# A two-layer diffusion trunk on one Trainium2 core: a shorter opening, 64-row products, and stationary expert weights

## The reference, cut to what matters

```python
def _trunk(x, cvec, P, caches):
    for l in range(DEPTH):
        mod = (jax.nn.silu(cvec) @ P['w_ada'][l] + P['b_ada'][l])[:, None, :]
        sh1, sc1, g1, sh2, sc2, g2 = jnp.split(mod, 6, axis=-1)
        mix, ctx_tensors = _token_mixer(x * (1.0 + sc1) + sh1, P, l, ctx)
        x = _layer_norm(DN_ALPHA * x + g1 * mix, P['ln1_g'][l], P['ln1_b'][l])
        h = x * (1.0 + sc2) + sh2
        f = _dense_ffn(h, P, l // 2) if l % 2 == 0 else _moe_ffn(h, P, l // 2)
        x = _layer_norm(DN_ALPHA * x + g2 * f, P['ln2_g'][l], P['ln2_b'][l])

def _moe_ffn(h, P, i):
    ...
    for e in range(N_EXPERTS):
        y = (jax.nn.silu(xt @ P['moe_w_gate'][i, e]) * (xt @ P['moe_w_up'][i, e])) @ P['moe_w_down'][i, e]
        out = out + gates[:, e:e + 1] * y
```

## Time and profile before

| | us |
|---|---|
| median of 3 runs (lowest, highest) | 2065.25 (2064.94, 2067.51) |
| the profiled execution | 2065.61 |
| its span, first to last instruction | 2063.8 |
| start of the first projection | 49.34 |
| start of the experts' weight transfers | 1144.25 |

### The profile page before, as it was taken

How to read it: one execution, slowest core, us unless ns; L and a number is a source line. 1 busy time by engine, 2 the same in 40 slices (tenths; PEclk the granted TensorE clock), 3 DMA queues, 4 the chain that set the end, 5 groups by cost and what they waited for, 6 DMA issues and landing times.

```text
span 2063.8 us, 25323 instructions
## 1 busy us (share of the span) xinstructions
PE 1962.5 (95%) x10904; PEld 1457.8 (71%) x10904; DVE 464.5 (23%) x984; ACT 253.3 (12%) x525; POOL 11.6 (1%) x24
## 2 busy tenths in 40 slices
PE   6999899998999989989998999999999999999996
PEld 3776668887888868788887766666666666577653
DVE  0244334222000033555333200000111000200103
ACT  0121113101000012221301100000000000000001
POOL 0000000000000000000000000000000000000000
PEclk8999999999999999999998899999999999999999
DMA  9436463323334343201230899999999999988794
GB/s 394 170 116 245 166 245 139 128 102 123 152 133 168 133 157 123 93 24 42 82 104 0 334 421 421 421 420 421 421 421 421 421 420 422 421 328 297 264 419 171
DMA packets 73565, 510.95 MB, mean 248 GB/s; under 512 B 9202, under 2 KB 10674, under 8 KB 11892
## 3 DMA queue, kind: packets, MB, share of 16 engines
q1 hardware_dynamic: 72820, 508.76, 62.3%
q0 software_dynamic: 640, 0.66, 0.1%
HBM read 507.68 MB, written 1.70 MB: 247 GB/s over the span
## 4 chain that ended last, share of the span: by engine, by line
PE 55%; DMA 5%; DVE 2%; ACT 0%; SPq 0%; issue 0%; ACTq 0%; DVEq 0%
PE bank L583 22%; PE bank L1037 10%; PE bank L1051 7%; DMA area<-in_moe 5%; PE bank L1061 5%; PE bank L904 3%; PE bank L788 1%; PE bank L773 1%; PE bank L1072 1%; PE bank L927 1%; PE bank L1044 1%; SPq L499 0%; PE bank L752 0%; PE bank L778 0%; PE bank L753 0%; DVE area L1463 0%
## 5 line engine op out<-in xcount | busy, mean ns | idle before, releaser
L583 PE MATMUL bank<-hT,area 128*128 128x256 f32 (+1 forms) x2080 | 460.8, 382 | 9.4 <-DVE hT L1468 9.4
L583 PEld LDWEIGHTS bank<-hT,area 128*128 128x128 f32 (+1 forms) x2080 | 392.4, 190 | 73.1 <-issue 11.5
L583 PE MATMUL bank<-area,mixer 128*128 128x256 f32 (+1 forms) x1408 | 309.5, 375 | 1.0 <-ACT mixer L1417 1.0
L583 PEld LDWEIGHTS bank<-area,mixer 128*128 128x128 f32 (+1 forms) x1408 | 256.5, 188 | 51.1 <-issue 20.6
L1037 PE MATMUL bank<-area,mixer 128*64 128x256 f32 x2240 | 255.2, 381 | 4.4 <-DMA area<-in_moe 4.4
L1037 PEld LDWEIGHTS bank<-area,mixer 128*64 128x64 f32 x2240 | 160.7, 137 | 97.9 <-issue 29.8
L1463 DVE TENSOR_TENSOR hT<-hT,bank 128x256 f32<-128x256 f32 x154 | 64.8, 421 | 717.4 <-ACT hT L1394 579.5
L1051 PE MATMUL bank<-area,hT 128*128 128x512 f32 x336 | 154.1, 601 | 0.5 <-ACT hT L1424 0.5
L1061 PE MATMUL bank<-area,hT 128*64 128x512 f32 x560 | 127.6, 597 | 2.7 <-DMA area<-in_moe 2.2
L1051 PEld LDWEIGHTS bank<-area,hT 128*128 128x128 f32 x336 | 61.4, 190 | 72.4 <-issue 71.0
L596 PE MATMUL bank<-area,cS 128*32 128x256 f32 x768 | 92.8, 398 | 18.9 <-DMA area<-in_ada 18.9
(11 more groups left out here) (290 smaller groups left out, 1430.3 us busy)
## 6 DMA issues: line engine op xcount, KB each, us to landing
area<-in_moe SPq DMA_DIRECT2D x336, 1024.0 KB, 24.0
area<-in_mix SPq DMA_DIRECT2D x62, 1024.0 KB, 4.9
area<-in_ada SPq DMA_DIRECT2D x48, 1024.0 KB, 6.8
area<-in_dense SPq DMA_DIRECT2D x33, 1024.0 KB, 6.7
cst<-in_cst SPq DMA_DIRECT2D x1, 2125.5 KB, 11.6
xT<-in_xT SPq DMA_DIRECT2D x1, 1024.0 KB, 21.0
out_yT<-xT SPq DMA_DIRECT2D x4, 256.0 KB, 2.5
mixer<-in_wbB SPq DMA_DIRECT2D x2, 256.0 KB
```

Of the source, the lines that this page charges most:

```text
L583: last = mm(out, a, b, start=(n == 0), stop=(n == len(pairs) - 1), **kw)
```

## The change

1. The opening takes 8 tiles of w_ada instead of 12. The other 40 are 20 early pairs: the two new ones are in stream 1 of layer 0, ahead of the wait for the decays and ahead of the wait for `nu_ready`. The ring's slots are counted on from there.
2. The constants come in two transfers: 8 columns in the opening, the rest behind the tiles q0 and q1.
3. The scores and the RWKV matrices are products over 64 rows, one for each half of the partitions, into different PSUM banks. The zeroed copies go; VectorE writes `KR` with two plain multiplications instead of four, and the start state for both heads side by side.
4. x takes the start state of two heads in one product; y alternates between the two column halves.
5. In wide expert passes the weights are stationary and the 128 gathered tokens move. The hidden values come out with a feature per partition, so the transposes and the copies to `mhidT` go, and down waits for `moe_hid`.

```diff
-ADA_FIRST = ADA_TILES // 2
+ADA_FIRST = ADA_TILES // 3
...
-            ada_first(0)
-            ada_first(1)
-            for name, dst in [("cst", cst), ("xT", xT), ("bada", bada), ("lnp", lnp), ("rv", rv)]:
...
+            for n in range(RING):
+                ada_first(n)
+            sp.dma_start(cst[:, 0:8], ins["cst"][:, 0:8]).then_inc(sem("cst_in"), 16)
+            for name, dst in [("xT", xT), ("bada", bada), ("lnp", lnp), ("rv", rv)]:
+                sp.dma_start(dst[:], ins[name]).then_inc(sem("params_in"), 16)
...
+                    if l == 0 and i == 2:
+                        sp.dma_start(cst[:, 8:], ins["cst"][:, 8:]).then_inc(sem("cst_in"), 16)
...
                 for j in range(4):
-                    mm(bank[4 + j][:, :], qL[:, j, :], kxL[:, :, :], start=True, stop=True)
+                    for g in range(2):
+                        mm(bk(4 + 2 * g + j // 2, 2, 256)[:, j % 2, :], qL[64 * g:64 * g + 64, j, :],
+                           kxL[64 * g:64 * g + 64, :], start=True, stop=True)
                 for j in range(4):
-                    last = mm(bk(2 + j // 2, 2, 256)[:, j % 2, :], qT[:, j, 0:P], kxP[:, :, :], start=True, stop=True)
+                    for g in range(2):
+                        last = mm(bk(2 + g, 4, P)[:, j, :], qT[64 * g:64 * g + 64, j, 0:P],
+                                  kT[64 * g:64 * g + 64, 0:P], start=True, stop=True)
...
+                elif l == 0:
+                    early_pair()
                 pe.wait_ge(sem("decays_ready"), 2 * k)
...
                     for c in range(2):
-                        mm(bank[2 + c][:, :], Bc[d][:, c, :], KR[d][:, c, :, :, :], start=True, stop=True)
-                        mm(bank[4 + c][:, :], KcR[d][:, c, :], KR[d][:, c, :, :, :], start=True, stop=True)
+                        for first, source in ((2, Bc), (4, KcR)):
+                            for i in range(2):
+                                half = slice(64 * i, 64 * i + 64)
+                                mm(bk(first + i, 2, 256)[:, c, :], source[d][half, c, :], KR[d][half, c, :, :],
+                                   start=True, stop=True)
                     for c in range(2):
                         for i in range(2):
-                            last = mm(bk(6, 4, P)[:, 2 * c + i, :], KR[d][:, c, 0, i, :], Bc[d][:, c, :],
+                            half = slice(64 * i, 64 * i + 64)
+                            last = mm(bk(6 + i, 2, P)[:, c, :], KR[d][half, c, 0, :], Bc[d][half, c, :],
                                       start=True, stop=True)
...
+                        if st == 1:
+                            mm(bank[2 + d][:, P * c:P * c + P], KR[d][:, c, 0, :], s0c[:, 2 * d + c, :, :],
+                               start=True, stop=False, skip_group_check=True)
...
+                if st == 1 and l == 0:
+                    early_pair()
                 pe.wait_ge(sem("nu_ready"), 2 * k)
...
+                    for d in range(2):
+                        for source, weights in ((Vn[:, st, :], AKQ[d]), (nU[d], MTQ[d])):
+                            for i in range(2):
+                                h = 2 * c + i
+                                last = mm(out[64 * i:64 * i + 64], source[:, 64 * h:64 * h + 64], weights[:, c, 1, i, :],
+                                          start=(st == 0 and d == 0 and source is not nU[d]),
+                                          stop=(d == 1 and source is nU[d]), skip_group_check=True)
...
-                    acc(out, [(x[:, c, :], m8(tile)[:, c, :]) for c in range(KC)]).then_inc(done, 1)
+                    for h in range(2):
+                        last = acc(out[:, P * h:P * h + P],
+                                   [(m8(tile)[:, c, P * h:P * h + P], x[:, c, :]) for c in range(KC)])
+                    last.then_inc(done, 1)
...
-                            last = mm(bank[first_bank + h][:, :], mhidT[par][:, P * c:P * c + P],
+                            last = mm(bank[first_bank + h][:, :], mhid[par][:, P * c:P * c + P],
...
-                        turn_hidden(u % 2).then_inc(sem("moe_turned"), 1)
+                        if not is_wide(q):
+                            pe.wait_ge(sem("moe_hid"), u + 1)
+                            turn_hidden(u % 2).then_inc(sem("moe_turned"), 1)
...
-                    for i in range(2):
-                        v.scalar_tensor_tensor(KR[d][:, :, 0, i, :], kapT[:, :, cols], hm[:, i:i + 1],
-                                               Ep[d][:, :, 1, :], ALU.mult, ALU.mult)
-                        v.scalar_tensor_tensor(KR[d][:, :, 1, i, :], rT[:, :, cols], hm[:, i:i + 1],
-                                               Ep[d][:, :, 0, :], ALU.mult, ALU.mult)
+                    mul(KR[d][:, :, 0, :], kapT[:, :, cols], Ep[d][:, :, 1, :])
+                    mul(KR[d][:, :, 1, :], rT[:, :, cols], Ep[d][:, :, 0, :])
```

More of the change, by code:

```diff
@@ L73, in add @@
         parts.append(a.astype(np.float32))
+    add("rows8", row == 32 * (np.arange(8)[None] // 2) + np.arange(8)[None] % 2)
     add("ident", row == col)
@@ L295, in m2, with mix_slot @@
             return moe_ring[:, s, :].rearrange("p (c n) -> p c n", c=2)
+        def mix_slot(l, i):
+            return (i + (ADA_FIRST if l == 0 else 0)) % RING
         fills = {}
@@ L302, in build_program @@
             for i, n in enumerate(MIX[l]):
-                count[i % RING] += 16
-                fills[(l, n)] = (i % RING, count[i % RING])
+                s = mix_slot(l, i)
+                count[s] += 16
+                fills[(l, n)] = (s, count[s])
             if l == 0:
@@ L378, in build_program @@
         unit_at = {u: n for n, u in enumerate(UNITS)}
+        narrow_at = {u: n for n, u in enumerate([u for u in UNITS if not is_wide(u[0])])}
         def nth_of_kind(tiles, n):
@@ L478, in unit_loads @@
                         l = int(kind == "moe")
-                        last = max(i for i in range(MIX_TILES[l]) if i % RING == s)
+                        last = max(i for i in range(MIX_TILES[l]) if mix_slot(l, i) == s)
                         sp.wait_ge(sem("tile_used"), MIX_BASE[l] + last + 1)
@@ L503, in _ @@
             for s in range(RING):
-                last = max(i for i in range(MIX_TILES[1]) if i % RING == s)
+                last = max(i for i in range(MIX_TILES[1]) if mix_slot(1, i) == s)
                 sp.wait_ge(sem("tile_used"), MIX_BASE[1] + last + 1)
@@ L791, in rwkv_stream @@
                     pe.wait_ge(sem(f"inv_T{d}"), k * LEVELS)
[L792 to L795, removed]
+                    for c in range(2):
                         if st == 1:
-                            pairs.append((KR[d][:, c, 0, i, :], s0c[:, 2 * d + c, :]))
-                        last = acc(out, pairs)
+                            mm(bank[2 + d][:, P * c:P * c + P], KR[d][:, c, 0, :], s0c[:, 2 * d + c, :, :],
+                               start=True, stop=False, skip_group_check=True)
+                        for i in range(2):
+                            h = 2 * c + i
+                            last = mm(bank[2 + d][:, 64 * h:64 * h + 64], AKQ[d][:, c, 0, i, :],
+                                      Vn[:, st, 64 * h:64 * h + 64], start=(st == 0), stop=True, skip_group_check=True)
                     last.then_inc(sem("x_done"), 1)
@@ L1405, in run @@
                         u = unit_at[(q, i)]
-                        act.wait_ge(sem("moe_turned"), u + 1)
-                        af(mhidT[u % 2], bank[2][:, 0:TW], ACT.Copy).then_inc(sem("moe_hidT"), 1)
+                        if not is_wide(q):
+                            act.wait_ge(sem("moe_turned"), narrow_at[(q, i)] + 1)
+                            af(mhidT[u % 2], bank[2][:, 0:TW], ACT.Copy).then_inc(sem("moe_hidT"), 1)
                         if groups is BEFORE:
@@ L1658, in rwkv_stream @@
                     dve.wait_ge(sem("mats_done"), 2 * (k - 1) + d + 1)
-                    mask = C(f"mask{d}").rearrange("p (x i t) -> p x i t", x=2, i=2)
-                    for c in range(2):
-                        mul(MTQ[d][:, c], bk(2 + c, 2, 2, P), mask)
-                    mul(Tm[d], bk(6, 4, P), over(C(f"lv0{d}"), 4))
-                    for c in range(2):
-                        last = mul(AKQ[d][:, c], bk(4 + c, 2, 2, P), mask)
+                    mask = C(f"mask{d}").rearrange("p (x i t) -> p x i t", x=2, i=2)[:, :, 0, :]
+                    mask = mask.unsqueeze(1).to_broadcast([P, 2, 2, P])
+                    for i in range(2):
+                        mul(MTQ[d][:, :, :, i, :], bk(2 + i, 2, 2, P), mask)
+                    for i in range(2):
+                        mul(Tm[d].rearrange("p (c i) t -> p c i t", c=2)[:, :, i, :], bk(6 + i, 2, P),
+                            over(C(f"lv0{d}"), 2))
+                    for i in range(2):
+                        last = mul(AKQ[d][:, :, :, i, :], bk(4 + i, 2, 2, P), mask)
                     chained(last)
```

88 lines of the change are left out of this document (38 added, 50 removed).

## The result

The changed kernel took 2029.86 us (median of four runs, 2028.43 to 2031.36), the kernel before beside it 2065.1. The ratio is 0.983, 95% interval 0.981 to 0.985. The forecast was 2033.4, its range 2019 to 2055. The profiled execution took 2031.36 us with a span of 2029.6, 34.2 less than before. Two of the four executions, this one among them, lie near 2031.2 us and two near 2028.5; the faster two have no profile.

What follows compares the result with a forecast made beforehand. TensorE was taken to bound the kernel, transfers the opening. Terms -15.0 (opening), +3.75 (pairs), -2.7 (scores), -14.3 (RWKV matrices), -5.6 (x and y), +2 (wide passes) sum to -31.85 us: from 2065.25 to 2033.4, range 2019 to 2055.

Steps and rivals of the forecast that it cites:

- What bounds the kernel: Whole kernel: TensorE, busy 95%; transfers bind the opening and cap savings in the experts at something like 10 us.
- The opening: Start of the kernel: 6.37 MB less ahead of the last w_ada pair gains 15.0 us, ends 13 and 17.
- The two pairs: Layer 0, stream 1: two more early pairs, one filling a wait, plus one more turn, add 3.75 us.
- The price 0.114: Scores and RWKV matrices: a 64-row product with 256 columns costs 0.114 us, as in column strips; bounds 0.108 and 0.216.
- The price 0.112: 128-column products, 64-row ones and wide passes: weight load rules, 0.112 us each; lower bound for 64 rows 0.056.
- The 0.2 per block: Scores and RWKV matrices: changing the array's split and back costs 0.2 us per block of 64-row products.
- RWKV matrices: Both layers' matrix blocks: 2.9 us each instead of 4.49 or 4.32, and slow blocks shorter; 14.3 us saved.
- x and y: RWKV stage: eight fewer x instructions and y alternating column strips save 2.8 us per layer, 5.6 in all.
- The wide passes: Experts: narrower products cost slightly more, two transposes go; net +0.05 us on 42 units, +2 us.
- Rival (b): Wide expert passes: weight loads exposed, 0.22 us a product, 290 us added, time about 2325; chance 0.07.
- Rival (a): Scores and RWKV matrices: the 64-row halves don't overlap, their savings become 0, time about 2050; chance 0.15.
- Rival (c): 64-row loads overlap (-5.4 us) and wide products run at 0.108 us (-11), time about 2017; chance 0.09.

Runs made afterwards that it cites:

- experiment 1: The changed kernel with the wide expert passes of the kernel before: tokens stationary, transposes and copies back; 2030.62 us.
- experiment 2: The changed kernel with all lower-half 64-row products issued before the upper-half ones in scores and RWKV matrix blocks; 2042.52 us.
- Experiment 5: The changed kernel with early pairs moved: two behind each layer 0 matrix block, the last four of the second stream dropped; 2023.23 us.
- experiment 6: The changed kernel with four unused products in TensorE's layer 1 gap, ahead of the second stream's first matrix block; 2025.87 us.
- experiment 9: The changed kernel, unaltered, run again for a second profile; 2030.76 us.
- Experiment 4: The changed kernel with ten unused products in TensorE's gap ahead of the last opening pair; 2027.28 us.
- experiment 3: The changed kernel with xT and the small parameters issued behind the eighth w_ada tile; 2025.37 us.
- experiment 10: The changed kernel with parameters behind the eighth tile, early pairs two behind each block and unused products in layer 1's gap, profiled a second time; 2014.15 us.
- experiment 8: The changed kernel with parameters behind the eighth tile, early pairs two behind each block and unused products in layer 1's gap, first run; 2011.53 us.

## Why the prediction was right

The forecast missed the time by 3.5 us, and its case, halves that overlap with wide passes at about the old price, is the one that came. Misses of opposite sign make the sum look better than its terms: those of the table come to about 17 us without their signs and to 2.4 with them. That the total came so close is in part luck.

**What bounds the kernel** was read rightly, and so was that transfers limit savings in the experts: TensorE's own work got 3.7 us shorter in the first stage, and the transfers took 2.9 of it back. The limit of 10 us was too wide by the prediction's own numbers: a stage of 632 us over 628 of transfers leaves 4.

**The opening** came out 2.8 us short. The last pair starts 15.0 us earlier (27.84 for 42.85), 1.1 less than the 16.1 of the transfers, and q0 follows its start by 9.26 us instead of 6.49. The prediction named both cases, a last pair at 3.65 us or behind a gap, and took the middle; the pair did fall behind the gap, and took 6.42, not the 5.57 of the pair in the earlier trace rows. The measured 12.2 lies outside the ends of 13 to 17. The end was too tight because it was priced by one row of a pair behind idle time. Five more profiles have this opening (experiments 1, 2, 5, 6 and 9): the pair takes 5.12 to 6.24 us behind 5.11 to 5.71 us of idle time, and q0 starts at 35.91 to 36.94, a gain of 12.4 to 13.4. Experiment 4 shows the cause, and experiment 3 that the place of `xT` in the queue was worth up to 5.6 us of the opening. That the constants behind q1 cost nothing held.

**The two pairs** were right in place and price: 3.6 for 3.75. Whether they could have been placed for less the prediction didn't ask: it read the 1.8 us waits behind the blocks only as a reason why a shorter block counts. Experiment 5 fills them with a pair each, at 0.7 and 2.3 us behind the first two.

**The price 0.114** for 64-row products with 256 columns came out to the digit: row halves cost here what column strips cost. **The price 0.112** for 128 columns is the step that failed: "no row shows a cheaper load of 128 columns" was true, and the row taken had loads of full height. The instructions take 0.061 to 0.068, so the sum was too dear by 16 x 0.051 = 0.8 us per layer in the scores and 8 x 0.044 = 0.35 per block. The Trainium skill, "TensorE: Matmul & The Clock Gate", Part 3, "The mechanism", said that loads for another row group are pulled ahead, so that such tiles overlap as wholes; the rows agree, with 0.061 to 0.068 nearer to the 0.056 that the prediction worked out by it than to the price that was taken. The 0.2 per block for the change of the array's split was too much as well: 1.83 and 0.54 us are the block's whole 2.37.

**RWKV matrices**: -17.1 for -14.3. A block is about 0.55 us shorter than forecast, which would make 4.3 us; 2.8 arrived. Most of the rest went to the groups behind the blocks: a gate of layer 1 takes 0.1 to 0.2 us longer than the 6.91 of before, the masking 0.1. The block behind layer 1's gap was expected at 5.0 and came at 4.57, and the clock was told rightly in both layers: full in layer 0, where the new pair fills the gap, low in layer 1. What was missed is that the gate behind it also loses 0.4 us more (7.49 against 7.10 in experiment 6). That experiment shows that the idle time is the cause.

**x and y** fell short by 0.8: in the first stream y gained 0.6 where 0.5 was counted, in the second x and y together 1.8 where 2.3 was.

**The wide passes**: the price of 0.112 was right to the third digit (7.14/64), the unit 10.58 for 10.61. What was counted as +2 came out as -1.3, since the wide unit's transposes had stood between two narrow strips: a wide and a narrow unit together fell from 21.77 to 21.5 us in the first stage where nothing else stands between those strips, which no step had looked at. Rival (b), the exposed loads, is excluded by that price, and experiment 1 reads the edit at 1.3 us. Rival (a) fell with the first block. Rival (c) was half right, on the 64-row loads.

**The slow projections** of layer 1, 3.2 us, no step foresaw; and the runs don't say whether the change is their cause.

## What to carry to other kernels

When a product uses half of the array's rows, price it by its own overlapping half, load included, and issue the halves in turn. An idle stretch can cost more than its length when short dense work stands behind it: read the first group after every gap for its clock, fill the gap with useful products or, failing that, with useless ones. Before placing extra work on the bounding engine, list its waits and put the work there; here that was worth 7.8 us of its stage, the whole change to the expert passes 1.3.

## What the hardware showed that was not expected

- TensorE's instructions over the two halves don't start in the order of issue: one of line 772 at 144.06, one of line 767, issued before it, at 144.27 (experiment 2).
- Products whose results nobody reads made a kernel faster: 3.7 us of them in an idle stretch gave back 2.6 us (experiment 6), 4.6 us of them 2.6 (experiment 4).
- A pair of tiles took 3.65 us at a granted clock of 1.00 behind 1.61 or 2.55 us of idle time (experiments 10 and 3), 6.56 at 0.54 behind 3.10 (experiment 8), 6.42 at 0.55 behind 5.01 (the changed kernel) and 5.12 at 0.70 behind 5.59 (experiment 5). The length of the idle time doesn't tell the price, and 1.25 us of later tiles became 4.2 us of later start.
- A busy stretch without any wait can run at a mean granted clock of 0.87 (805 to 818 us, kernel after), in a place that can differ from one execution of a program to another (experiments 8 and 10).
